# Moving the start addresses of the matmul operands of a two-block transformer kernel to multiples of 256 bytes in a partition

## Time and profile before

| | us |
|---|---|
| three runs, median (lowest to highest) | 1658.75 (1657.31 to 1665.09) |
| profiled execution | 1662.15 |
| its span | 1660.6 |
| mean granted TensorE clock in it | 0.958 |

### The profile page before, as it was taken

The page is one execution under the profiler, slowest core; times in us unless marked ns, Lnnn a source line. Parts: engine busy times, 40 slices in busy tenths (PEclk is TensorE's granted clock), DMA queues, the critical chain, the costliest instruction groups (busy, mean ns, idle before and its releaser), DMA issues.

```text
span 1660.6 us, 27694 instructions
## 1 busy us (share of the span) xinstructions
PE 1544.9 (93%) x10710; PEld 1419.5 (85%) x10710; DVE 1083.1 (65%) x1590; ACT 727.3 (44%) x835; POOL 313.8 (19%) x306
## 2 busy tenths in 40 slices
PE   5998889899999999998999999998999897689997
PEld 5977679799999999997888888878998795589986
DVE  5544466679999988845555555567774575577743
ACT  4334454344445445444444444444343356243431
POOL 2000000000010111114766767620000010000000
PEclk8999889999999999999999999998999996899999
DMA  6542214457667578786888888864555440245551
GB/s 246 185 176 96 77 61 161 152 170 250 217 230 231 191 255 289 261 289 242 292 291 284 296 285 285 289 235 142 180 180 176 175 166 26 89 146 196 183 185 63
DMA packets 56291, 329.65 MB, mean 199 GB/s; under 512 B 7473, under 2 KB 7521, under 8 KB 24721
## 3 DMA queue, kind: packets, MB, share of 16 engines
q1 hardware_dynamic: 35856, 259.01, 44.7%
q0 software_dynamic: 20352, 69.47, 12.2%
HBM read 294.90 MB, written 33.55 MB: 198 GB/s over the span
## 4 chain that ended last, share of the span: by engine, by line
PE 89%; DVE 5%; ACT 3%; issue 2%; DMA 1%; DVEq 0%; ACTq 0%; SPq 0%
PE ub L1506 17%; PE ub L1508 16%; PE ub L1507 16%; PE acc L1506 11%; PE acc L1508 11%; PE acc L1507 11%; PE acc L1693 3%; DVE wl L861 1%; ACT wh L526 1%; DMA raw<-in_wstream 1%; PE acc L1571 1%; PE acc L1470 1%; PE ub L1595 0%; DVE rstd L878 0%; PE mb L1581 0%
## 5 line engine op out<-in xcount | busy, mean ns | idle before, releaser
L861 DVE TENSOR_TENSOR wl<-raw,wh 128x2048 fp32r<-128x2048 f32 x245 | 565.4, 2309 | 291.2 <-ACT wh L526 289.8
L1506 PE MATMUL ub<-xh,wh 128*128 128x256 f32 x2216 | 633.6, 286 | 18.8 <-DVE wl L861 6.7
L1508 PE MATMUL ub<-xh,wl 128*128 128x256 f32 x2216 | 626.2, 283 | 0.0
L1507 PE MATMUL ub<-xl,wh 128*128 128x256 f32 x2216 | 626.1, 283 | 0.0
L526 ACT CAST wh<-raw 128x2048 fp32r<-128x2048 f32 x245 | 467.0, 1907 | 222.6 <-DMA raw<-in_wstream 85.4
L1506 PEld LDWEIGHTS ub<-xh,wh 128*128 128x128 f32 x2216 | 423.9, 191 | 22.1 <-DVE wl L861 20.4
L1508 PEld LDWEIGHTS ub<-xh,wl 128*128 128x128 f32 x2216 | 424.3, 191 | 0.0
L1507 PEld LDWEIGHTS ub<-xl,wh 128*128 128x128 f32 x2216 | 423.6, 191 | 0.1
L1506 PE MATMUL acc<-wh,ah 128*128 128x512 f32 x512 | 200.3, 391 | 6.2 <-issue 6.2
L1507 PE MATMUL acc<-wl,ah 128*128 128x512 f32 x512 | 200.1, 391 | 0.0
L1508 PE MATMUL acc<-wh,al 128*128 128x512 f32 x512 | 200.1, 391 | 0.0
(11 more groups left out here) (315 smaller groups left out, 1650.8 us busy)
## 6 DMA issues: line engine op xcount, KB each, us to landing
raw<-in_wstream SPq DMA_DIRECT2D x245, 1024.0 KB, 4.9
gates<-gst POOLq DMA_DIRECT2D x16, 1024.0 KB, 14.9
gl_in<-gates POOLq DMA_DIRECT2D x64, 256.0 KB, 3.1
hidden<-hid POOLq DMA_DIRECT2D x60, 256.0 KB, 5.3
hid<-hidden POOLq DMA_DIRECT2D x60, 256.0 KB, 3.0
resid<-in_x SPq DMA_DIRECT2D x2, 512.0 KB, 4.0
rb<-in_rel POOLq DMA_DIRECT2D x1, 1024.0 KB, 10.3
wb<-in_ffn_post_g POOLq DMA_DIRECT2D x2, 512.0 KB, 3.9
```

What stands on the lines that cost most here:

```text
L861: v.tensor_tensor(wl[:, slot, :], raw[:, slot % RAW, :], wh[:, slot, :].bitcast(F32), ALU.subtract).then_inc(w_low, 1)
L1506: pe.matmul(dst, sh, mh, start=first, stop=False)
L1507: pe.matmul(dst, sh, ml, start=False, stop=False)
L1508: return pe.matmul(dst, sl, mh, start=False, stop=last)
```

## The change

It moves start addresses and nothing else: no instruction is added, removed or put elsewhere, and no shape changes.

```diff
+        sb("shift_w", [P, 32])
         raw = sb("raw", [P, RAW, CW])
         wh = sb("wh", [P, RING, CW], F32R)
         wl = sb("wl", [P, RING, CW], F32R)
         resid = sb("resid", [P, TT, D])
-        sb("shift_x", [P, 16])
         xh = sb("xh", [P, KD, T], F32R)
...
-        sb("shift_y", [P, 24])
+        sb("shift_y", [P, 40])
...
-        sb("shift_q", [P, 24], at=st2)
+        sb("shift_q", [P, 40], at=st2)
         qkT = sb("qkT", [P, 24, T], at=st2)
...
-        sb("shift_o", [P, 24], at=st2)
+        sb("shift_o", [P, 40], at=st2)
         odh = sb("odh", [P, KD, T], F32R, at=st2)
```

## The result

The changed kernel takes 1676.41 us (median of 4 runs, 1675.76 to 1678.66), the kernel before beside it 1658.49 (4 runs, 1657.31 to 1665.09). The ratio is 1.0093 [1.007, 1.0115]: about 0.9% slower. The forecast was 1588 with a range to 1640. What came is the rival on the slower side, in sign, in size (+14, 1673 us) and in its price per matmul.

What follows compares the result with a forecast made beforehand. TensorE's matmul cost was taken as the bound, with 89% of the chain of waits. Stage savings summed to 71.3 us, lowering the median from 1658.75 to 1587.5, say 1588 us, range 1574 to 1640.

Steps and rivals of the forecast that it cites:

- the rival on the slower side: Equal start remainders of both operands collide: 120 ns per unit (256-column) matmul, +14 us, 1673 us; chance 0.12.
- I take 109.2 and 215.8: Assumed ns per fp32r matmul of 256 and 512 columns once all operands start at remainder 0.
- The bounds: Matmul price limits: below 106.7 / 213.3 ns, columns at full clock; above 120 ns for a unit, 226.7 for a wide one.
- differ by 4 ns in nothing but the start address of the moving side: Reading of 256-column matmuls with `xh` moving (117.8 ns) and `odh` moving (113.6 ns), taken to show addresses cost time.
- The objection that kept the rival at 0.12: Against colliding equal remainders: two pairs at the same distance lose 6.9 and 20 ns, so distance alone does not order rows.
- 1 to 4, 6, 7, 9, 11: Projections, attention, gate and plain chunks, feed-forward first products, mixer, wo: savings 7.0, 1.6, 2.9, 1.3, 12.1, 3.3, 17.2, 2.5 plus 0.9 us.
- 8 and 10: PEER's second half and the feed-forwards' second products: 10.9 ns less per `ah`/`fh` matmul, saving 16.7 and 5.8 us.
- the 17.5: Saving in ns claimed for each 512-column matmul with `xh` stationary.
- The bf16 spreads: In the 24 gate chunks, bf16 operands going from 128 to 0: between 0 and 768 x 6.7 = 5.1 us, 2.2 taken.
- stage 3: bd, bc and out: 288 `odh`/`och` units at 4.2 ns and 96 `xh` wide matmuls at 17.5 ns, saving 2.9 us.
- Stage 5: PEER's first 32 chunks: VectorE sets the end; 3 us gained, 3 charged for lost clock, net 0.
- One seventeenth is fixed: Rival: fp32r reading costs 17/16 anywhere, units 113.3 ns, `xh` wide 226.7; saves 26.6 us, 1632 us; chance 0.27.

Runs made afterwards that it cites:

- map1: Only fp32r matmuls in a row, the rest of the computation left out, at chosen start remainders: 113.3 to 120.0 ns at 256 columns, 227.2 to 233.3 at 512.
- map2: Only matmuls in a row: 8-byte distance steps, a 64-column stationary side, 384 moving columns, varied predecessors; 256-column matmuls with 128 stationary columns cost 113.4 to 121.8 ns.
- map3: Only matmuls in a row: fp32r with 32 or 96 stationary columns, alternating distances, then bf16; bf16 took 109.2 ns at 256 columns at all eight distances.
- w_only: Kernel before with the weights' side alone moved to 0 (raw, wh, wl, resid): 1659.66 us against 1660.96, ratio 0.9987.
- zero_less64: Changed kernel with only the moving sides (xh, xl, odh, odl, och, ocl) put at 192, weights staying at 0: 1641.64 us against 1661.32, ratio 0.9878.
- x_sixtyfour: Kernel before with xh and xl moved from 192 to 64, 64 below the weights: 1645.88 us, ratio 0.9882.
- x_equal: Kernel before with xh and xl moved from 192 to 128, the weights' remainder: 1675.51 us against 1663.97, ratio 1.0066.
- x_zero: Kernel before with xh and xl alone moved to 0, weights staying at 128: 1668.57 us, ratio 1.0042.

## Why the prediction was wrong

**The step that failed** is "I take 109.2 and 215.8". It carried the floor of plain float32 (a pass costs its columns plus 2.5 ns) over to fp32r, on the ground that reading would no longer be late at remainder 0. Reading at 0 is not special (map1), and fp32r does not get under 113.3 and 226.6 at any distance tried. The bounds were right: the upper end, "120 ns for a unit matmul and 226.7 for a wide one", is to the digit what came, but the range to 1640 was not drawn from it. I chose the lower end because one row lay near it, and that row was of another data type. It also had its two sides at equal remainders, one width and one pair of starts, so it could not say what a pass costs "at any remainder"; the plain float32 matmuls of 128 columns in map2 take 111.7 ns a record over 106.7, 5 ns and not 2.

**The step behind it** read the earlier trace rows one side at a time: units and `odh` "differ by 4 ns in nothing but the start address of the moving side". True, and the distance differed with it. Four rows cannot tell two sides and a distance apart unless one asks for it. Read by d they agree with map1's price list: at 256 columns 64 gives 117.8 and 192 gives 113.3, at 512 columns 0 gives 226.7 (227.2 in map1) and 192 gives 233.3. The row for d = 0 at 256 columns, which the change makes all units be, was missing.

**The objection that kept the rival at 0.12** was "64 below (stationary 128, moving 64) costs 6.9 and (192, 128) costs 20, the same distance". That compared a 256-column row with a 512-column row. map1 shows that the two shapes have different prices at one distance: at d = 192 the excess is 6.6 and 20.0 ns, at d = 0 it is 13.3 and 13.9. The 13.4 ns carried to the units was right because at d = 0 these two widths happen to agree; at 384 columns it is 15.0. So the rival had the sign, the price and the condition right, and its reason is not shown. It says that the loss comes from the stationary side being loaded and is the same at every width. At 256 columns and d = 0 half a load left 10.0 of 13.3 ns and a quarter of it left 11.0. At 512 columns and d = 0 the price even rose, from 227.2 with 128 stationary columns to 230.6 with 64 and 231.1 with 32. That two operands' starts decide together is shown; how they get in each other's way is open.

**By stages.** 1 to 4, 6, 7, 9, 11: the units were mis-sized, +2.2 instead of -8.6. 8 and 10, 22.5 us of the forecast, are zero: `ah`/`fh` was at d = 0 already. `xh` wide gained 6.6 of the 17.5. The bf16 spreads, 2.2 us taken, gained nothing: 24 of them fill 1.60 us of the chain at the first spread before and 1.54 after, 48 of them 3.00 and 3.03 at the last; bf16 shows no effect of the distance in map3 either. In stage 3 the `odh`/`och` units went up by 6.7 where 4.2 was to come off. Stage 5: the argument that VectorE would set the end was not put to the test in the changed kernel, where TensorE got slower and VectorE's waits for `wh` grew from 6.5 to 9.3 us. Where units got faster it held: in w_only TensorE waited for VectorE at the first spread, and the stage gave back 3.6 us where "I take 3" stood; in zero_less64 VectorE's share of the chain rose from 5% to 14%.

**What held.** Addresses cost time in fp32r. They cost none at half clock (213.3 ns between units there, before and after). Plain float32 did not move: 215.8 ns a record on line 1768 before (192, 192) and after (64, 64), and in map2 111.7 ns with the moving start at 0, 64, 128 and 192. Line 963 and the remainder on line 861 (2306 ns, before 2309) don't care. DMA held 1% of the chain in both kernels. The rival *One seventeenth is fixed* was right that no fp32r row of 256 or 512 columns is under 113.3 and 226.6, and wrong that the changed kernel's units reach it: at 256 columns d = 192 does, and d = 64 now and then.

## What to carry to other kernels

For fp32r matmuls look at the distance between the starts of the two operands, not at their alignment. With 128 stationary columns the best found was moving less stationary = 192 (mod 256) for 256 moving columns and 0 for 512. At 256 columns avoid 0: it cost 119.4 to 120.0 ns in every run that had it. A good distance is no promise, since the same addresses came out at either of two prices in different stretches, so the whole kernel has to be timed. bf16 showed no such effect, nor did plain float32.

A price read at one data type or width is not to be carried to another. Where the price sought has no row, a kernel of nothing but that matmul over all distances gives it in half a millisecond. And when several rows differ in two addresses, tabulate their difference too before calling one of them the cause.

## What the runs showed of the hardware

- An fp32r matmul's cost goes with d = (moving start - stationary start) mod 256 bytes. With 128 stationary columns it is 113.3 to 120.3 ns at 256 columns in steps of 32 bytes, and up to 121.8 in steps of 8. At 512 columns it is 226.7 to 234.6 in steps of 32, and up to 238 in steps of 8.
- Several distances have more than one price with the same addresses. At 256 columns d = 192 and d = 64 have 113.3 and 117.8 ns (map1, map2, x_sixtyfour, zero_less64, w_only, x_equal), and d = 128 runs from 118.0 to 120.0 (x_zero). At 512 columns d = 64 has 229 (w_only) and 233.3 (zero_less64), and d = 0 has 226.7 (the kernels) to 229.9 (map2). In the kernels a price is kept while TensorE runs without a gap and can change at the next resumption after other work. At d = 192 the two are worth up to 6500 x 4.5 ns = 29 us of this kernel. What selects one is not shown.
- At 384 columns and 128 stationary ones all eight distances took 173.1 to 176.9 ns, over 160.
- fp32r is not seen under 17/16 of the column time (113.3, 226.6), bf16 is (109.2, 215.9). A matmul of fp32r always brings its own load here, so whether the load is the cause could not be separated.
